# First two feed-forward blocks: eight of the 22 gate and up pairs in each as seven block products

## The chip, the cores and the metric

The kernel runs on one core of a Trainium2 chip. The metric is the device time of one execution in microseconds; smaller is better. TensorE (PE in the profile) multiplies matrices into eight PSUM banks, VectorE (DVE), ScalarE (ACT) and GpSimd (POOL) do the elementwise work, and the queue of SyncE (SP) starts the weight loads.

## The reference, cut to what matters

The program is a chain of transformer-like blocks over 512 tokens of width 1024: a state-space mixer, a feed-forward block, a differential attention, a second feed-forward block, a three-branch mixer, a cross attention, and a third feed-forward block. The change touches the first two feed-forward blocks, which have a short causal convolution over the tokens between the projection and the gate:

```python
def conv_ffn(x, ln_g, up_w, conv_w, conv_b, down_w):
    u = causal_dwconv(rms_norm(x, ln_g) @ up_w, conv_w, conv_b)   # 3 taps
    gate, up = u[..., :FFN_DIM], u[..., FFN_DIM:]                 # FFN_DIM = 2816
    return (jax.nn.silu(gate) * up) @ down_w
```

The third block has the same gate and up projections with no convolution. 2816 columns are 22 tiles of 128, so each block has 22 pairs: one gate tile and one up tile, each a product of a 1024x128 weight with the 1024x512 transposed activations.

## The kernel before, in words

**Order.** A planner (`Plan`) writes out one order of work by hand in ticks. A tick is one piece of TensorE work; every engine's program walks over the same ticks and does what the planner placed there, in order, so each engine is a strict queue whose entries carry an age in ticks. A wait in the middle of a queue holds all that stands behind it.

**Precision.** Each float32 product is made of three float32r products of a rounded high part and a low rest: `wl*xh + wh*xl + wh*xh`. Each unit of weights (128x1024) is loaded by SP into one of three raw buffers, rounded on ACT (`split`, line 1715) and its rest subtracted on DVE (`cut`, line 2230); TensorE waits for the `cut` of the unit (`features`, `quads`).

**An ordinary pair** (`feat` twice) takes 8 ticks: gate in 4 pieces of 6 matmuls of 512 columns, then up likewise, 48 matmuls. Two units are cut. In the first two blocks DVE scales each finished bank into a padded buffer `fu` (`scaled`), ACT makes the first convolution tap of it into `fv`, DVE adds taps 1 and 2 (`SCALAR_TENSOR_TENSOR`, line 2233), ACT makes the silu of the gate, POOL multiplies gate and up (line 2877; DVE for tiles 11 and 21), ACT rounds the result and DVE subtracts the rest (`two_parts`) for the down projection.

**A quad** (`quad`) takes 7 ticks of 12 matmuls of 256 columns, 84 matmuls: a pair regarded as a 2x2 block product (gate and up by the two halves of the 1024 rows; the two halves of the rows by the two halves of the tokens) done by Strassen's seven products p1, p2, p6, p5, p7, p3, p4. Before the change only eleven pairs of the third block are quads. A quad needs four weight units instead of two: the gate weights, two sums of weight blocks (`s1`, `s2`, four additions of 128x512 on DVE at ticks -5 and -3) and half of the up weights. It also needs four combinations of activation blocks ("tees", 4 chunks, made once per block). Its products share three banks: a, b and d. ACT copies the bank b after p1 and after p6, and the bank d after p5, before TensorE may go on in them; DVE reads the bank b after p7 (`q_read`) before p4 may go in.

The waits of TensorE inside a quad are, in `quads`, `cut` of the unit for each product, and

```python
if product == "p6":
    w.wait_ge(*sig["q_copy"].at(f, "p1"))
elif product == "p7":
    w.wait_ge(*sig["q_copy"].at(f, "p6"))
elif product == "p3":
    w.wait_ge(*sig["q_copy"].at(f, "p5"))
elif product == "p4":
    w.wait_ge(*sig["q_read"].at(f))
```

Cut units live in a ring of three buffers. The third unit of a quad, `s2`, is split on ACT in tick 1 of the quad and cut on DVE in tick 2, since its buffer is that of the unit that TensorE left at the end of the tick before the quad; p7 needs it in tick 4.

Of the kernel before, what the change touches and what calls it, by code (L numbers as in the profile page):

```python
# [9 lines left out]
F = mybir.dt.float32  # L10
# [143 lines left out]
QUADS = (4, 5, 7, 8, 10, 12, 13, 15, 16, 18, 19)  # L154
# [7 lines left out]
class Plan:  # L162
# [132 lines left out]
    def quad(self, f, gate, gate_c, up, up_c):  # L295

        key = ("gu", 2, f)
        self.until(lambda: self.past("tees", 3, 6) and self.place(
# [4 lines left out]
        g = Group(key, False, "n2", 0, [], DC, 0, P, H2)  # L303
        sources = (("raw", r, 0, UNIT), ("s1", f, 0, UNIT), ("s2", f, 0, UNIT), ("raw", r + 1, S, S))
# [7 lines left out]
        self.quad_units[f] = (r, *g.units)  # L312
        for u, end in zip(g.units, (("bank", (*key, "a")), ("product", (f, "p5")), ("bank", (*key, "d")),
                                    ("bank", (*key, "b")))):
            self.unit_end[u] = end
        self.start("sum1", f, t - 5)
        self.start("sum2", f, t - 3)
        self.start("quad", f, t)
        src, i = h_of(2, f)
        self.lo[src, i] = t + 11  # L320
# [568 lines left out]
class Buffers:  # L889


    def __init__(self, nc, ctx):
# [41 lines left out]
        self.teeh, self.teel = (t[:, :, :].rearrange("p (i c) (h n) -> p i (c h) n", i=4, h=2) for t in (self.XBh, self.XBl))  # L934
# [126 lines left out]
class Kernel:  # L1061
# [52 lines left out]
    def raw_read(self, r):  # L1114
# [140 lines left out]
def tensor_program(eng, K):  # L1255
# [45 lines left out]
    def quads(p):  # L1301

        g, product = p.group, PRODUCTS[p.k0]
        f = g.key[2]
# [7 lines left out]
        if product == "p6":  # L1312
            w.wait_ge(*sig["q_copy"].at(f, "p1"))
        elif product == "p7":
            w.wait_ge(*sig["q_copy"].at(f, "p6"))
        elif product == "p3":
            w.wait_ge(*sig["q_copy"].at(f, "p5"))
        elif product == "p4":
            w.wait_ge(*sig["q_read"].at(f))
        for k in range(4):  # L1320
            if product == "p1":
                xh, xl = (t[:, 0:H2] for t in buf.operand("n2", k))
                w.wait_ge(*K.ready("n2", k))
            elif product in ("p2", "p3"):
                xh, xl = (t[:, 0:H2] if product == "p2" else t[:, H2:S] for t in buf.operand("n2", 4 + k))
                w.wait_ge(*K.ready("n2", 4 + k))
            else:
                i = ("p5", "p6", "p7", "p4").index(product)
                xh, xl = buf.teeh[:, i, k, :], buf.teel[:, i, k, :]
                w.wait_ge(*sig["tee_lo"].at(k, i))  # L1330
# [3 lines left out]
        t.then_inc(*(fill(key) if QUAD_LAST[name] == product else sig["product"].up(f, product)))  # L1334
# [372 lines left out]

def scalar_program(eng, K):
# [18 lines left out]
    def values(g):  # L1727

        for j in range(g.n):
# [19 lines left out]
            if o == in_bank - 1:  # L1749
                t.then_inc(*leave(key))  # L1750

    ADDED = {"nf": ("out", 3), "nq": ("dn", 0, 1), "nf1": ("ao", 1), "nm": ("dn", 1, 1), "nx": ("mo",), "n2": ("xo", 1),
             "fin": ("dn", 2, 1)}
# [156 lines left out]
    def tees(T):  # L1910
        for k in at("tees", T):
            x_ready("n2", k)
            w.wait_ge(*full(("rs", "n2")))
            w.wait_ge(*sig.par.at())
            if k:
                for i in range(4):
                    w.wait_ge(*sig["tee_lo"].at(k - 1, i))
            copy(K.tee(0), buf.x[:, k, H2:S], pc("ffn2", k)).then_inc(*sig["tee_d"].up(k))
        for k in at("tees", T - 2):
            w.wait_ge(*full(("xo", 1, DC - 1)))  # L1920
            for i, sign in enumerate((1.0, -1.0, 1.0, -1.0)):
                w.wait_ge(*K.tee_ready(k, i))
                copy(buf.teeh[:, i, k, :], K.tee(1 + i), sign).then_inc(*sig["tee_hi"].up(k, i))

    def quads(T):
        for product, age in (("p1", 1), ("p6", 3), ("p5", 4)):
            for f in at("quad", T - age):
                vg, vu = K.quad_rows(f)
                w.wait_ge(*sig["product"].at(f, product))
                if product == "p1":  # L1930
                    w.wait_ge(*K.gated(2, f - 3))
                if product == "p5":
                    w.wait_ge(*sig["lo"].at(*h_of(2, f - 3)))
                out = {"p1": vg[:, 0:H2], "p6": vg[:, H2:S], "p5": vu[:, H2:S]}[product]
                copy(out, K.of(("gu", 2, f, QUAD_BANK[product]))[:, 0:H2]).then_inc(*sig["q_copy"].up(f, product))
        for f in at("quad", T - 7):
            vg, _ = K.quad_rows(f)
            w.wait_ge(*sig["q_row"].at(f))
            func(ACT.Silu, vg[:, :], vg[:, :]).then_inc(*sig["fsilu"].up(2, f))
        for f in at("quad", T - 9):  # L1940
            src, i = h_of(2, f)
            hi, _ = buf.operand(src, i)
            w.wait_ge(*K.gated(2, f))
            if f >= 12:
                w.wait_ge(*full(("dn", 2, 0, DC - 1)))
# [1219 lines left out]
```

## Time and profile before

| | |
|---|---|
| median of 3 runs | 2399.07 us (2397.6 to 2399.99) |
| the profiled execution's own time | 2399.27 us |
| its span, first to last instruction | 2397.5 us |
| PE busy | 2371.2 us, 99% |
| DVE busy | 1484.8 us, 62% |
| ACT busy | 1086.1 us, 45% |
| POOL busy | 357.9 us, 15% |
| TensorE's granted clock, mean | 0.998 of full speed |

An engine is busy while an instruction of its own executes. The span lacks 1.8 us of the execution's time, which lie ahead of the first and behind the last instruction. Shares are means over all stages; what a stage is limited by is read from its own window.

### The profile page before, as it was taken

The page shows a single profiled execution, that of the slowest core. Times are in us where ns is not written, and L with a number is a line of the kernel's source. Part 1 is how long each engine was busy: PE and PEld are TensorE (multiplying, and loading weights), DVE is VectorE, ACT ScalarE, POOL GpSimd, SP SyncE. Part 2 cuts the span into 40 slices and gives each one's busy share as a digit, 9 for nine tenths or more (in the row PEclk, how much of TensorE's full clock was granted, in tenths as well). Part 3 has the DMA queues.
Part 4 walks back from the last instruction along what each step waited for, and adds up shares of the span by engine and source line. Part 5 has one row for each costly group of instructions (what it writes and reads, how often), then busy time and mean ns, then how long its engine had stood idle before and what let it go on. Part 6 is the DMA issues. An engine that isn't in the chain of part 4 may idle for free.

```text
span 2397.5 us, 30764 instructions
## 1 busy us (share of the span) xinstructions
PE 2371.2 (99%) x11952; PEld 1944.2 (81%) x11952; DVE 1484.8 (62%) x2356; ACT 1086.1 (45%) x1878; POOL 357.9 (15%) x286
## 2 busy tenths in 40 slices
PE   8999999999999999999999999999999999999999
PEld 6677878888888877788888877787788878898987
DVE  6778776763666777766456547534655445873763
ACT  6654554442445677644234334324443334442433
POOL 0252252210111000122011100001210001100001
PEclk9999999999999999999999999999999999999999
DMA  4532223223223221232332332231234332233232
GB/s 164 109 93 79 80 70 99 97 86 108 97 83 120 75 76 49 73 108 92 93 106 87 91 131 84 71 102 57 72 123 136 115 106 79 81 105 99 95 97 89
DMA packets 74847, 226.24 MB, mean 94 GB/s; under 512 B 8144, under 2 KB 12368, under 8 KB 74576
## 3 DMA queue, kind: packets, MB, share of 16 engines
q1 hardware_dynamic: 70272, 215.90, 28.1%
q10 hardware_dynamic: 4432, 8.39, 2.0%
q8 instruction: 95, 1.56, 0.3%
q14 instruction: 48, 0.39, 0.1%
HBM read 215.87 MB, written 8.39 MB: 94 GB/s over the span
## 4 chain that ended last, share of the span: by engine, by line
PE 60%; DVE 1%; ACT 0%; issue 0%; DMA 0%; POOL 0%; POOLq 0%; DVEq 0%; ACTq 0%; SPq 0%
PE bank L1272 59%; PE bank L1276 1%; DVE t L2230 1%; DVE t L2233 1%; ACT t L1715 0%; DVE t L2241 0%; DMA t<-in_w 0%; POOL t L2877 0%; ACT t L1718 0%; ACT L1718 0%; DVE t L2237 0%; DVE t L2798 0%; POOLq L3100 0%; DVEq L3100 0%; DVE t L2644 0%
## 5 line engine op out<-in xcount | busy, mean ns | idle before, releaser
L1272 PE MATMUL bank<-t 128*128 128x512 f32 (+5 forms) x11526 | 2346.4, 369 | 19.1 <-DVE t L2233 7.9
L1272 PEld LDWEIGHTS bank<-t 128*128 128x128 f32 (+2 forms) x11526 | 1901.0, 186 | 433.3 <-issue 80.1
L1715 ACT ACTIVATE t<-t 128x1024 fp32r<-128x1024 f32 (+5 forms) x676 | 564.0, 847 | 564.6 <-PE bank L1272 276.6
L2230 DVE TENSOR_TENSOR t<-t 128x1024 fp32r<-128x1024 f32 (+7 forms) x774 | 687.3, 901 | 202.9 <-ACT t L1715 192.4
L1718 ACT ACTIVATE t<-t 128x512 f32<-128x512 f32 (+6 forms) x610 | 367.5, 616 | 455.8 <-DVE t L2230 307.1
L2877 POOL TENSOR_TENSOR t<-t 128x512 f32<-128x512 f32 (+4 forms) x206 | 316.3, 1542 | 1551.9 <-ACT t L1718 559.7
L2230 DVE TENSOR_TENSOR t<-bank,t 128x512 f32<-128x512 f32 (+4 forms) x434 | 279.2, 648 | 425.2 <-PE bank L1272 414.7
L2233 DVE SCALAR_TENSOR_TENSOR t<-t 128x512 f32<-128x512 f32 (+5 forms) x536 | 386.6, 733 | 102.3 <-ACT t L1718 63.8
L1715 ACT ACTIVATE t<-bank 128x512 f32<-128x512 f32 (+4 forms) x184 | 84.7, 477 | 205.4 <-PE bank L1276 146.9
L2880 POOL TENSOR_SCALAR t<-t 128x128 f32<-128x128 f32 (+3 forms) x64 | 40.9, 645 | 478.6 <-ACT t L1715 247.6
L2233 DVE SCALAR_TENSOR_TENSOR t<-bank,t 128x512 f32<-128x512 f32 x56 | 38.5, 688 | 68.8 <-PE bank L1272 68.8
L1276 PE MATMUL bank<-t 128*128 128x128 f32 (+1 forms) x426 | 69.1, 277 | 1.9 <-ACT t L1715 1.2
L1718 ACT ACTIVATE t<-bank,t 128x128 f32<-128x128 f32 (+1 forms) x144 | 42.3, 392 | 44.9 <-DVE t L2798 39.2
L2233 DVE SCALAR_TENSOR_TENSOR t<-t,bank 128x512 f32<-128x512 f32 x40 | 28.4, 710 | 54.2 <-PE bank L1272 51.7
L2241 DVE CUSTOM_DVE_ANT_0 t<-bank,t 128x256 f32<-128x256 f32 (+3 forms) x128 | 55.7, 462 | 9.8 <-PE bank L1272 7.5
L1276 PEld LDWEIGHTS bank<-t 128*128 128x128 f32 (+1 forms) x426 | 50.0, 141 | 14.4 <-issue 4.2
L1718 ACT ACTIVATE t<-bank 128x512 f32<-128x512 f32 (+3 forms) x73 | 38.5, 539 | 13.4 <-PE bank L1272 8.5
L2237 DVE TENSOR_SCALAR t<-t 128x256 f32<-128x256 f32 (+6 forms) x88 | 33.6, 383 | 2.9
L1715 ACT ACTIVATE t<-bank,t 128x256 f32<-128x256 f32 (+1 forms) x32 | 15.3, 524 | 21.9 <-PE bank L1272 18.7
L1718 ACT ACTIVATION_READ_ACCUMULATOR t<-t 128x1 f32 x128 | 24.4, 191 | 0.0
L1718 ACT ACT_TABLE_LOAD x11 | 14.1, 1283 | 0.2
L2238 DVE TENSOR_SCALAR t<-bank 128x4 f32<-128x4 f32 (+1 forms) x14 | 2.2, 159 | 16.8 <-PE bank L1272 16.8
(30 smaller groups left out, 53.0 us busy)
## 6 DMA issues: line engine op xcount, KB each, us to landing
t<-in_w SPq DMA_DIRECT2D x304, 512.0 KB, 3.4
t<-in_w SPq DMA_DIRECT2D x48, 384.0 KB, 3.0
t<-in_w SPq DMA_DIRECT2D x56, 320.0 KB, 3.0
t<-in_w SPq DMA_DIRECT2D x28, 256.0 KB, 2.8
tab<-t ACTq DMA_DIRECT2D x1, 2560.0 KB
t<-in_x SPq DMA_DIRECT2D x8, 256.0 KB, 5.0
t<-tab SPq DMA_DIRECT2D x8, 256.0 KB, 3.7
spill<-t ACTq DMA_DIRECT2D x1, 2048.0 KB, 8.3
```

The lines of the kernel that those rows point to most:

```text
L1272: return eng.matmul(out, lhs, rhs, start=start, stop=stop, skip_group_check=loose)
L1276: return eng.transpose(out, in_, ident[0:n, 0:n])
L1715: return eng.activation(out, in_, ACT.Copy, scale=scale)
L1718: return eng.activation(out, in_, f, bias=bias, scale=scale, accum_out=accum)
L2230: return eng.tensor_tensor(out, a, b, o)
L2233: return eng.scalar_tensor_tensor(out=out, in0=a, scalar=s, in1=b, op0=o0, op1=o1)
L2237: return eng.tensor_scalar(out, a, s0, None, o0)
L2238: return eng.tensor_scalar(out, a, s0, s1, o0, o1)
L2241: return eng.tensor_tensor_reduce(out, a, b, 1.0, FMAX, ADD, MIN, m)
L2877: return eng.tensor_tensor(out, a, b, o)
L2880: return eng.tensor_scalar(out, a, s, s1, o, o1)
```

## The change

Pairs 5, 7, 9, 12, 14, 16, 18 and 20 of blocks 0 and 1 become quads; the third block keeps its eleven. So between two new quads stands one ordinary pair (two before the down projections of tiles 0 to 11, pairs 10 and 11). The combinations of activations are made for the first two blocks too, in the 4 MB (XAh, XAl) that are free there, with 6 ticks from chunk to chunk (4 in the third block). The convolution stays in a quad: DVE scales the assembled rows into `fu` (the up half with a factor -1), then ACT and DVE make the taps for gate and up, DVE makes the product of gate and up that POOL makes for an ordinary pair.

```diff
-QUADS = (4, 5, 7, 8, 10, 12, 13, 15, 16, 18, 19)
+QUADS = {0: (5, 7, 9, 12, 14, 16, 18, 20), 1: (5, 7, 9, 12, 14, 16, 18, 20), 2: (4, 5, 7, 8, 10, 12, 13, 15, 16, 18, 19)}
...
-        self.lo[src, i] = t + 11
+        self.lo[src, i] = t + (11 if s == 2 else 14)
...
-        if s == 2:
-            for k in range(4):
-                self.once("tees", k, lambda k=k: self.past("rms", "n2", 3) and (k == 0 or self.past("tees", k - 1, 4)))
+        apart = 4 if s == 2 else 6
+        for k in range(4):
+            self.once("tees", (s, k), lambda k=k: self.past("rms", src, 3) and (
+                k == 0 or self.past("tees", (s, k - 1), apart)))
...
-                if s == 2 and f in QUADS:
-                    self.quad(f, gate, gate_c, up, up_c)
+                if f in QUADS[s]:
+                    self.quad(s, f, gate, gate_c, up, up_c)
                     continue
...
-        self.teeh, self.teel = (t[:, :, :].rearrange("p (i c) (h n) -> p i (c h) n", i=4, h=2) for t in (self.XBh, self.XBl))
+        self.tees = [tuple(t[:, :, :].rearrange("p (i c) (h n) -> p i (c h) n", i=4, h=2) for t in pair)
+                     for pair in ((self.XAh, self.XAl), (self.XAh, self.XAl), (self.XBh, self.XBl))]
```

On ACT, in `quads`:

```diff
+        for kind, age in (("ga", 7), ("up", 8)):
+            for s, f in at("quad", T - age):
+                if s == 2:
+                    continue
...
+                w.wait_ge(*(sig["q_row"] if kind == "ga" else sig["q_up"]).at(s, f))
...
+                func(ACT.Identity, buf.fv[n % 6][:, :], buf.fu[n % 3][:, 2:S + 2], pc(f"fcb{s}", ft),
+                     pc(f"fcw{s}", 3 * ft)).then_inc(*sig["tap0"].up((kind, s, f)))
+        for age in (10, 7):
+            for s, f in at("quad", T - age):
+                if age == (10 if s < 2 else 7):
...
+                    func(ACT.Silu, vg[:, :], vg[:, :]).then_inc(*sig["fsilu"].up(s, f))
+        for age in (12, 9):
...
+                    copy(hi, K.quad_rows(f)[1][:, :], 1.0 if s < 2 else -1.0).then_inc(*sig["hi"].up(src, i))
```

On DVE, in `quads`:

```diff
+            if s < 2:
+                fu_free(2 * f, s)
+                tt(buf.fu[2 * f % 3][:, 4:S + 4], vg[:, :], row[:, :], MUL).then_inc(*sig["q_row"].up(s, f))
...
+            if s < 2:
+                out = buf.fu[(2 * f + 1) % 3][:, 4:S + 4]
+                fu_free(2 * f + 1, s)
+                stt(out[:, H2:S], vu[:, H2:S], -1.0, row[:, H2:S], MUL, MUL).then_inc(*sig["q_up"].up(s, f))
+                w.wait_ge(*full(("gu", s, f, "b")))
+                stt(out[:, 0:H2], b, -1.0, row[:, 0:H2], MUL, MUL).then_inc(*leave(("gu", s, f, "b")))
...
+        for kind, age in (("ga", 8), ("up", 9)):
+            for s, f in at("quad", T - age):
+                if s < 2:
+                    taps((kind, s, f))
+        for age in (11, 8):
+            for s, f in at("quad", T - age):
+                if age == (11 if s < 2 else 8):
...
+                    tt(vu[:, :], vu[:, :], vg[:, :], MUL).then_inc(*sig["fmul_last"].up(s, f))
+        for age in (13, 10):
...
+                    if s < 2:
+                        tt(lo, K.quad_rows(f)[1][:, :], hi.bitcast(F), SUB).then_inc(*sig["lo"].up(src, i))
...
+    def taps(key):
...
+        for k in (1, 2):
+            w.wait_ge(*(sig["tap0"].at(key) if k == 1 else sig["tap"].at(key, 1)))
+            stt(v[:, :], ub[:, 2 + k:S + 2 + k], pc(f"fcw{s}", 3 * ft + k), v[:, :], MUL, ADD).then_inc(
+                *sig["tap"].up(key, k))
```

## Rows read from the trace of the kernel before

**Rows 1.** The page: span, engines, granted clock, chain that ended last

```profile
span 2397.5 us, 30764 instructions
...
PE 2371.2 (99%) x11952; PEld 1944.2 (81%) x11952; DVE 1484.8 (62%) x2356; ACT 1086.1 (45%) x1878; POOL 357.9 (15%) x286
...
PEclk9999999999999999999999999999999999999999
...
PE 60%; DVE 1%; ACT 0%; issue 0%; DMA 0%; POOL 0%; POOLq 0%; DVEq 0%; ACTq 0%; SPq 0%
```

**Rows 2.** Critical chain in time order, first-block stretch: start us, us, what

```profile
1033.38 360.24 PE bank L1272 x1592
```

**Rows 3.** Windows: us, PE, PEld, DVE, ACT, POOL busy, PEclk, DMA share, GB/s

```profile
1060.00:1125.30 65.30, 65.30 (x290) 54.07 (x289) 44.00 (x55) 28.84 (x38) 13.23 (x6) 1.00 0.31 98
2228.00:2240.00 12.00, 12.00 (x101) 11.90 (x100) 9.70 (x16) 6.80 (x11) 0.00 (x0) 1.00 0.29 89
2257.40:2288.60 31.20, 31.20 (x217) 29.20 (x216) 26.18 (x37) 14.48 (x22) 1.68 (x1) 1.00 0.33 102
```

**Rows 4.** DVE groups by form, 440 to 505.28 us (first block, ordinary pairs)

```profile
L2233 DVE SCALAR_TENSOR_TENSOR t<-t 128x512 f32<-128x512 f32 x25 | 18.8, 752 | 7.8 <-ACT t L1718 7.3
L2230 DVE TENSOR_TENSOR t<-t 128x1024 fp32r<-128x1024 f32 x12 | 14.6, 1219 | 0.0
```

**Rows 5.** DVE groups by form, 2226.2 to 2288.6 us (third block, two periods)

```profile
L2230 DVE TENSOR_TENSOR t<-t 128x512 f32<-128x512 f32 x24 | 17.2, 730 | 1.1
L2230 DVE TENSOR_TENSOR t<-bank,t 128x256 f32<-128x256 f32 x16 | 6.7, 420 | 4.5 <-PE bank L1272 4.5
L2230 DVE TENSOR_TENSOR t<-bank,t 128x512 f32<-128x512 f32 x4 | 2.8, 688 | 3.5 <-PE bank L1272 3.5
```

**Rows 6.** DVE in time, first block: start us, us, what, xcount, idle before

```profile
477.87 1.54 DVE L2233 SCALAR_TENSOR_TENSOR t<-t 128x512 f32<-128x512 f32 x2 [0.22 <-ACT t L1718]
479.32 1.22 DVE L2230 TENSOR_TENSOR t<-t 128x1024 fp32r<-128x1024 f32 x1
```

**Rows 7.** DVE, then POOL, in time, third block

```profile
2258.27 2.39 DVE L2230 TENSOR_TENSOR t<-t 128x512 f32<-128x512 f32 x2
...
2270.88 1.22 DVE L2230 TENSOR_TENSOR t<-t 128x1024 fp32r<-128x1024 f32 x1
2272.01 0.68 DVE L2233 SCALAR_TENSOR_TENSOR t<-t 128x512 fp32r<-128x512 f32 x1
...
2258.44 1.68 POOL L2877 TENSOR_TENSOR t<-t 128x512 f32<-128x512 f32 x1 [116.19 <-DVE t L2230]
```

**Rows 8.** ACT groups by form, 2226.2 to 2288.6 us

```profile
L1715 ACT ACTIVATE t<-t 128x1024 fp32r<-128x1024 f32 x16 | 16.6, 1047 | 0.0
L1715 ACT ACTIVATE t<-bank 128x256 f32<-128x256 f32 x12 | 4.6, 383 | 15.1 <-PE bank L1272 15.1
```

**Rows 9.** ACT groups by form, 440 to 505.28 us

```profile
L1718 ACT ACTIVATE t<-t 128x512 f32<-128x512 f32 x18 | 13.6, 754 | 18.7 <-DVE t L2230 14.3 <-DVE t L2233 3.9
```

**Rows 10.** All engines in time, entry into the third block's first quad

```profile
2083.06 7.25 PEld L1272 LDWEIGHTS bank<-t 128*128 128x128 f32 x60 [1.87 <-DVE t L2230]
```

**Rows 11.** DVE in time, one chunk of tees' low parts, third block

```profile
2066.60 1.42 DVE L2233 SCALAR_TENSOR_TENSOR t<-t 128x256 fp32r<-128x256 f32 x4
```

**Rows 12.** DVE in time, ordinary pair of the first block

```profile
476.95 0.69 DVE L2230 TENSOR_TENSOR t<-t 128x512 fp32r<-128x512 f32 x1
```

**Rows 13.** DMA issues by line: size of one, median us to landing

```profile
t<-in_w SPq DMA_DIRECT2D x304, 512.0 KB, 3.4
```

More of the change, by code:

```diff
@@ L293, in feat_steps, with quad @@
         self.pending.append(g)
-    def quad(self, f, gate, gate_c, up, up_c):
-        key = ("gu", 2, f)
-        self.until(lambda: self.past("tees", 3, 6) and self.place(
+    def quad(self, s, f, gate, gate_c, up, up_c):
+        key = ("gu", s, f)
+        self.until(lambda: self.past("tees", (s, 3), 6) and self.place(
             [((*key, "b"), 0, 10), ((*key, "a"), 1, 4), ((*key, "d"), 3, 6)]), key)
@@ L311, in quad @@
             self.put(Piece(g, i // 2, i, i + 1, i == 0))
-        self.quad_units[f] = (r, *g.units)
-        for u, end in zip(g.units, (("bank", (*key, "a")), ("product", (f, "p5")), ("bank", (*key, "d")),
+        self.quad_units[s, f] = (r, *g.units)
+        for u, end in zip(g.units, (("bank", (*key, "a")), ("product", (s, f, "p5")), ("bank", (*key, "d")),
                                     ("bank", (*key, "b")))):
             self.unit_end[u] = end
[L316 to L319, printed above, removed]
-        self.lo[src, i] = t + 11
+        self.start("sum1", (s, f), t - 5)
+        self.start("sum2", (s, f), t - 3)
+        self.start("quad", (s, f), t)
+        src, i = h_of(s, f)
+        self.lo[src, i] = t + (11 if s == 2 else 14)
     def halves(self, key, name, c, src, nk, row0, per, after):
@@ L1910, in tees @@
     def tees(T):
-        for k in at("tees", T):
-            x_ready("n2", k)
-            w.wait_ge(*full(("rs", "n2")))
+        for sk in at("tees", T):
+            s, k = sk
+            src = FFN_IN[s]
+            x_ready(src, k)
+            w.wait_ge(*full(("rs", src)))
             w.wait_ge(*sig.par.at())
@@ L1916, in tees @@
                 for i in range(4):
[L1917 to L1920, printed above, removed]
+                    w.wait_ge(*sig["tee_lo"].at((s, k - 1), i))
+            copy(K.tee(0), buf.x[:, k, H2:S], pc(GAINS[src], k)).then_inc(*sig["tee_d"].up(sk))
+        for sk in at("tees", T - 2):
+            s, k = sk
+            teeh, _ = buf.tees[s]
+            w.wait_ge(*full((*ADDED[FFN_IN[s]], DC - 1)))
@@ L1936, in quads @@
[L1936 to L1945, printed above, removed]
-            copy(hi, K.quad_rows(f)[1][:, :], -1.0).then_inc(*sig["hi"].up(src, i))
+                copy(out, K.of(("gu", s, f, QUAD_BANK[product]))[:, 0:H2]).then_inc(*sig["q_copy"].up(s, f, product))
@@ L2505, in quads @@
             w.wait_ge(*K.loaded(r + 1))
[L2506 to L2512 removed]
+            if before:
+                w.wait_ge(*sig["cut"].at(before[2]))
@@ L2513, in quads @@
+            tt(buf.s1[:, S:UNIT], b[:, 0:S], b[:, S:UNIT], ADD).then_inc(*sig["sum1"].up(sf))
+            w.wait_ge(*sig["sum1"].at(sf))
+            tt(buf.s1[:, 0:S], a[:, 0:S], buf.s1[:, S:UNIT], ADD).then_inc(*sig["sum"].up(*sf, "s1"))
+        for sf in at("sum2", T):
+            r, before = plan.quad_units[sf][0], K.sums_before(sf)
             a, b = buf.raws[r % N_W], buf.raws[(r + 1) % N_W]
-            if f != QUADS[0]:
-                w.wait_ge(*sig["cut"].at(plan.quad_units[QUADS[QUADS.index(f) - 1]][3]))
+            if before:
+                w.wait_ge(*sig["cut"].at(before[3]))
@@ L2524, in quads @@
-        for f in at("quad", T - 5):
+            w.wait_ge(*full(("gu", s, f, "a")))
+            w.wait_ge(*sig["q_copy"].at(s, f, "p1"))
+            tt(vg[:, 0:H2], K.of(("gu", s, f, "a"))[:, 0:H2], vg[:, 0:H2], ADD).then_inc(*leave(("gu", s, f, "a")))
+        for s, f in at("quad", T - 5):
             _, vu = K.quad_rows(f)
-            w.wait_ge(*sig["product"].at(f, "p7"))
-            w.wait_ge(*sig["q_copy"].at(f, "p5"))
-            tt(vu[:, H2:S], K.of(("gu", 2, f, "b"))[:, 0:H2], vu[:, H2:S], ADD).then_inc(*sig["q_read"].up(f))
@@ L2529, in quads @@
[L2529 removed]
+            w.wait_ge(*sig["product"].at(s, f, "p7"))
+            w.wait_ge(*sig["q_copy"].at(s, f, "p5"))
+            tt(vu[:, H2:S], K.of(("gu", s, f, "b"))[:, 0:H2], vu[:, H2:S], ADD).then_inc(*sig["q_read"].up(s, f))
+        for s, f in at("quad", T - 6):
             vg, _ = K.quad_rows(f)
[L2531 to L2537 removed]
@@ L2551, in quads @@
-        for f in at("quad", T - 10):
-            src, i = h_of(2, f)
-            hi, lo = buf.operand(src, i)
-            w.wait_ge(*sig["hi"].at(src, i))
-            stt(lo, K.quad_rows(f)[1][:, :], -1.0, hi.bitcast(F), MUL, SUB).then_inc(*sig["lo"].up(src, i))
+            row = K.rms_row(FFN_IN[s])
+            w.wait_ge(*full(("gu", s, f, "d")))
+            tt(vg[:, H2:S], K.of(("gu", s, f, "d"))[:, 0:H2], vg[:, H2:S], ADD).then_inc(*leave(("gu", s, f, "d")))
+            w.wait_ge(*empty(("rb", FFN_IN[s])))
```

194 lines of the change are left out of this document (106 added, 88 removed).

## The prediction

> **What bounds the kernel now.** I read the page first: PE is busy 99% of the span at full clock, and the chain that ended last runs over PE's matmuls; DVE has 62%, ACT 45%, POOL 15% [rows 1]. The chain in order of time then shows that the feed-forward stretch is one unbroken run of matmuls [rows 2]. So time falls only if TensorE gets less to do, and rises as soon as TensorE waits. The windows give its prices. In the first block's ordinary pairs 65.30 us hold 290 matmuls of 512 columns, one or two of them only overlapping the edges: 0.2267 us each. In a quad of the third block 12.00 us hold 101 of 256 columns: 0.120 us each [rows 3]. The same rows show the other side: DVE is busy 44.00 of 65.30 us in ordinary pairs (67%), and 26.18 of 31.20 us (84%) where two quads and a pair alternate [rows 3].
>
> **What TensorE saves.** A pair costs 48 x 0.2267 = 10.88 us, a quad 84 x 0.120 = 10.08 us, so 0.80 us are saved each, 12.8 us over 16. A matmul of half the columns costs 53%, not 50%, and there are 7/8 of the columns.
>
> The Trainium skill (TensorE: Matmul & The Clock Gate, section "Wait — 56ns, not 53.3ns?") puts a warm matmul at its columns by 2.4 GHz plus some 2.5 ns. By that a pair would be 10.36 us and a quad 9.17 us, and the saving 19 us, an estimate from that page; the rows disagree (226.7 and 120 ns against 215.8 and 109.2), and since both forms are measured here, in this kernel's own loops, the rows decide.
>
> **What DVE gets to do.** I take a period of one new quad and one ordinary pair, 15 ticks: TensorE needs 10.08 + 10.88 = 20.96 us. DVE's part:
> - Ordinary pair: 44.00 / 6 = 7.33 us [rows 3]. It holds two cuts of 1.22 us, four taps of 0.75 [rows 4], two evictions of 0.69 [rows 5] and the rest of 0.69 [rows 12]; neighbours overlap by 0.08. The two taps of a bank take 1.45 us from start to next start, 1.42 of it busy [rows 6]; without taps the pair is 7.33 - 2.84 = 4.49.
> - POOL's product of gate and up, once a period: while it ran in the third block, two DVE instructions of 512 took 2.39 us together [rows 7], where 2 x 0.69 less the overlap is 1.3. So it costs a loaded DVE 1.05 us; the mean of 24 such, 730 against 688 ns [rows 5], says the same.
> - Quad of the third block: (26.18 - 4.49 - 1.05) / 2 = 10.32 us. Three and a half cuts, four additions for the sums, three additions of 256 columns, scaling, product and rest are in it.
> - The new quads add the taps of gate and up, 2.84 us: 13.16. Their product of gate and up is on DVE in the third block as well. The form with a factor of -1 takes the place of a plain one; no row here has it with a bank of 256 columns, and between a plain one of 0.42 [rows 5] and a tap of 0.75 for twice the columns [rows 4] the difference is under 0.1 us each; I take 0, and 0.2 a period for the high end.
>
> Sum: 13.16 + 7.33 + 1.05 = 21.54 us of busy DVE, 103% of TensorE's 20.96. DVE becomes the bound of the alternating stretches. Two forced idles come on top. After the eviction of the up bank DVE has one addition (0.33) to do before it needs ACT's first tap (0.75 [rows 9]): 0.35 with the semaphores. After the gate row it has two of 256 (0.7) against ACT's 0.75: 0.1. So a period is 22.0 us, and a saturated one stalls TensorE for 22.0 - 20.96 = 1.05 us. Before, two pairs took 21.76.
>
> **Where TensorE waits.** The tight entry is the cut of `s2`: its buffer comes free only as the quad begins, and p7 needs it in tick 4, 4 x 12 x 0.120 = 5.76 us later. In the first new quad DVE is on time. From its tick 8 (11.3 us, when the gate row and the first tap are there) to tick 13 the queue holds, from start to next start, two times taps and cut (2.58 each), sums (1.3 and 1.27), eviction and product (1.27), rest, taps and cut (3.2): 12.2 us. It ends at 23.5, 2.55 into the next quad. Then eviction 0.61, ACT's tap 0.75, taps 1.45, cut 1.13 and some 0.05: 6.55 against 5.76. Quad 7 stalls 0.8, quad 9 1.05. The first quad behind the down projections, 12, has no pair ahead whose taps it must carry, so 14 stalls 0.35 and 16, 18, 20 stall 1.05 each. That is 1.85 + 3.5 = 5.35 per block, 10.7 for both. After 9 and after 20 a lag remains of under 3 us; pairs 10 and 11, where DVE is at 67%, and the missing sums behind quad 20 take it in: 0.
>
> **The other edits.** The four chunks of tees are eight DVE operations of 256 each: four rests take 1.42 us [rows 11], four combinations as much, so 2.9 a chunk, 11.4 a block, ahead of quad 5. TensorE's pairs leave DVE 3.55 us each, 17.7 in five, so they fit, but with the first evictions, that come in one lump, up to 1 us of lag reaches quad 5. In the third block the first quad's start waited 1.87 us for DVE [rows 10], with 4 ticks between chunks and two quads in a row; here I take 0.5 per block, 1.0 in all (0 to 3.8). ACT gets 1.5 splits of 1.05 us and three copies of 0.38 more per quad [rows 8]; with 44% of its time used in ordinary pairs [rows 3] it reaches some 55%, hidden by itself, but it stands in the same chain: its copy of p1 is queued behind the silu that waits for DVE's taps, and by the ledger above ends 0.1 to 0.3 us before p6 needs it. If that cover goes, the price is the same lag, not a second one. Weight loads stay the same bytes; a load of 3.4 us [rows 13] is started when DVE has cut or summed a buffer, some 7 us ahead of its next use, since no two new quads are neighbours. The down projection gets its operand three ticks later in the plan, with a pair behind every quad. All 0.
>
> **Sum.** -12.8 + 10.7 + 1.0 = -1.1 us against the profiled execution's 2399.27 (span 2397.5 [rows 1]); that time is 0.2 above the median of the runs shown, so 2398.0 on its scale: no change that can be told, since about 0.2%, 4.8 us, is what a measurement of this kernel can tell from none.
>
> **Rivals.**
> - *DVE keeps up (faster).* Without POOL's 1.05 the busy time is 20.5, below 20.96, and the idles fall in the 0.5 left. For it: TensorE lost only 31.20 - 168 x 0.120 - 48 x 0.2267 = 0.16 us in a period of two quads at 84% [rows 3], and POOL may fall where DVE waits anyway. Against: in the saturated queue the cut of half a unit and its like follow POOL's start at once. Stalls would be 16 x 0.08 and 1.0 at the entries, 2.3: 12.8 - 2.3 = 10.5 us faster, 2388.6. It decides below 20.96 of DVE per period. Chance 0.30. The Trainium skill (SBUF — State Buffer, "Who interferes with whom") says that GpSimd and a DVE instruction with two SBUF inputs lock each other out for the whole instruction, and that one with a single SBUF input is free; the 2.39 us agree. By that rule POOL costs nothing if additions out of banks follow it, which is this rival.
> - *ACT and DVE wait for each other (slower).* The mechanism is the chain in two strict queues: POOL's late product holds ACT's rounding, behind which stands the split of the next unit, which DVE's cut waits for (0.2 to 0.4 us), besides dependent neighbours (0.04 each, five of them) and the longer form with -1 (0.2). The period is then 22.8: saturated stalls 1.84, the first ones 0.8 longer: 3.4 + 6.7 per block, 20.2 for both, and 1.0: 8.4 us slower, 2407.5. It decides from some 1.5 us per saturated stall. For it: with 84% DVE still idled for ACT and TensorE in turn. Chance 0.22.
> - *The entries cost what the third block's does.* 3.8 instead of 1.0: 2400.8. Chance 0.04, on top of the forecast's 0.44.
>
> **How the numbers follow.** The forecast's own range is a period of 21.7 to 22.3 us, 12 x 0.3 = 3.6 us either way, 2394.5 to 2402. The 8-in-10 range takes in both rivals' numbers, 2388.5 to 2408. Faster by over 0.2% is the first rival and the low edge of the forecast: 0.32; within 0.45; slower 0.23.
>
> **What the profile after would show.** PE: 1344 more matmuls of 256 columns and 768 fewer of 512. In pairs 14 to 20 of the first two blocks DVE busy above 95%, with waits of TensorE for DVE (the cut, before p7) of about 1 us per quad, none of that size in quads 5 and 12. Four to six waits of ACT in a row would speak for the second rival; DVE under 92% and stalls of 0.1 for the first. I am wrong if TensorE's waits come from ACT's copies, from the loads, or from the entry.

## The result and the profile after

The changed kernel takes 2413.19 us in the median (4 runs, 2412.21 to 2414.16), the kernel before 2399.53 beside it (4 runs, 2397.6 to 2400.66): a ratio of 1.006, 95% interval 1.0045 to 1.0075. It is slower by 13.7 us, outside the predicted range of 2388.5 to 2408.

The page of the changed kernel, the same parts as [rows 1]:

```profile
span 2411.7 us, 32441 instructions
...
PE 2366.2 (98%) x12528; PEld 1965.2 (81%) x12528; DVE 1616.3 (67%) x2596; ACT 1133.2 (47%) x1998; POOL 325.0 (13%) x270
...
PE 53%; DVE 7%; ACT 1%; issue 1%; DMA 0%; POOL 0%; DVEq 0%; POOLq 0%; ACTq 0%; SPq 0%
```

PE has 576 matmuls more, as was worked out, and 5 us less of busy time where 12.8 were: part of TensorE's waiting is counted as busy, as the sums below show. DVE now holds 7% of the chain that ended last, where it held 1%. DVE is busy 131 us longer.

Who TensorE waited for, in the whole span (engine and line, total us, times, longest):

```profile
PE bank L1281 <- DVE t L2262: 22.6, 19, 2.9
```

L2262 is the line of the cut and of DVE's other operations on two inputs (L2230 before); 17 of the 19 waits, 19.8 us, are in blocks 0 and 1. A block's length can be read from the starts of its matmuls, since their number is known. Blocks 0 and 1 took 359.8 and 359.9 us before and 366.9 and 367.2 after; the attention in between 255.9 and 255.8. So the two blocks hold the loss, 14.4 us; the other stages vary by up to 1.5 us between kernels in which they are the same.

Windows of the changed kernel, as [rows 3]: the stretch from pair 0 to the entry of quad 7, then single periods of a new quad and a pair:

```profile
417.50:482.60 65.10, 60.26 (x304) 51.02 (x303) 60.90 (x91) 36.31 (x59) 11.15 (x5) 1.00 0.26 81
672.50:694.90 22.40, 21.38 (x134) 19.23 (x134) 21.26 (x30) 11.68 (x18) 2.20 (x1) 1.00 0.29 94
1295.30:1317.70 22.40, 21.38 (x135) 19.22 (x134) 21.26 (x31) 11.68 (x18) 2.20 (x1) 1.00 0.30 95
```

A period is 22.4 us with 21.26 us of busy DVE, against 22.0 and 21.54 predicted. The first window is the surprise: DVE is busy 60.90 of 65.10 us before the alternation has begun. The kernel before in the same stretch:

```profile
417.30:482.60 65.30, 65.30 (x292) 54.12 (x290) 47.20 (x58) 30.96 (x40) 12.63 (x6) 1.00 0.29 93
```

So DVE's first pairs were fuller than the 44.00 us of [rows 3] already. Ahead of quad 5 alone, 43.4 us from 417.5, DVE was idle for 11.0 us before and is for 3.1 after. TensorE's waits in that stretch stand in the order of time (start us, us, what, idle before):

```profile
439.73 14.67 PE L1281 MATMUL bank<-t 128*128 128x512 f32 x64
455.29 8.56 PE L1281 MATMUL bank<-t 128*128 128x512 f32 x48 [0.89 <-DVE t L2262]
466.76 3.13 PE L1281 MATMUL bank<-t 128*128 128x256 f32 x24 [2.92 <-DVE t L2262]
470.93 4.34 PE L1281 MATMUL bank<-t 128*128 128x256 f32 x34 [1.04 <-DVE t L2262]
```

From the starts of the matmuls these waits are worth 1.1, 3.1 (ahead of p6) and 1.4 us with the slower matmuls right behind each: 5.6 per block. Quads 7, 9, 16, 18 and 20 wait 1.39 us each, all but 0.1 of it ahead of p7, quad 14 0.73, quad 12 nothing: 7.7 per block. So 26.6 us of waits in two blocks stand against 12.8 us saved. (The trace counts 19.8 of the 26.6 as idle, the rest as busy.)

### The profile page after: what moved, and what is told of

Read it like the earlier page. It is cut to its first block, busy times and chain, and to the rows that moved or that the text cites. A ratio compares the mean times of both kernels' runs of the same rounds, so it can differ in the third digit from the quotient of the medians.

```text
span 2411.7 us, 32441 instructions
## 1 busy us (share of the span) xinstructions
PE 2366.2 (98%) x12528; PEld 1965.2 (81%) x12528; DVE 1616.3 (67%) x2596; ACT 1133.2 (47%) x1998; POOL 325.0 (13%) x270
## 4 chain that ended last, share of the span: by engine, by line
PE 53%; DVE 7%; ACT 1%; issue 1%; DMA 0%; POOL 0%; DVEq 0%; POOLq 0%; ACTq 0%; SPq 0%
PE bank L1281 52%; DVE t L2262 4%; DVE t L2265 3%; PE bank L1285 1%; ACT t L1733 1%; ACT t L1730 0%; DVE t L2273 0%; DMA t<-in_w 0%; POOL t L2945 0%; ACT L1733 0%; DVE t L2269 0%; DVE t L2866 0%; POOLq L3168 0%; DVEq L3168 0%; DVE t L2712 0%
## 5 line engine op out<-in xcount | busy, mean ns | idle before, releaser
L1281 PE MATMUL bank<-t 128*128 128x512 f32 (+3 forms) x12102 | 2341.7, 359 | 38.4 <-DVE t L2262 22.6
L1281 PEld LDWEIGHTS bank<-t 128*128 128x128 f32 (+1 forms) x12102 | 1922.4, 187 | 426.7 <-issue 82.6
L2262 DVE TENSOR_TENSOR t<-t 128x1024 fp32r<-128x1024 f32 (+8 forms) x902 | 792.3, 897 | 197.1 <-ACT t L1730 184.5
L1730 ACT ACTIVATE t<-t 128x1024 fp32r<-128x1024 f32 (+8 forms) x748 | 603.5, 824 | 565.2 <-PE bank L1281 269.2
L2262 DVE TENSOR_TENSOR t<-bank,t 128x512 f32<-128x512 f32 (+3 forms) x450 | 276.0, 620 | 339.2 <-PE bank L1281 327.3
L2945 POOL TENSOR_TENSOR t<-t 128x512 f32<-128x512 f32 (+3 forms) x190 | 283.5, 1500 | 1600.5 <-ACT t L1733 578.0
L2265 DVE SCALAR_TENSOR_TENSOR t<-t 128x512 f32<-128x512 f32 (+3 forms) x616 | 423.1, 703 | 76.7 <-ACT t L1733 37.3
L1730 ACT ACTIVATE t<-bank 128x256 f32<-128x256 f32 (+4 forms) x232 | 102.6, 455 | 219.3 <-PE bank L1285 145.2
L2265 DVE SCALAR_TENSOR_TENSOR t<-bank,t 128x512 f32<-128x512 f32 (+1 forms) x72 | 45.2, 628 | 67.2 <-PE bank L1281 67.2
L1285 PEld LDWEIGHTS bank<-t 128*128 128x128 f32 (+1 forms) x426 | 49.7, 140 | 14.2 <-issue 3.9
L1733 ACT ACTIVATE t<-bank 128x512 f32<-128x512 f32 (+3 forms) x73 | 38.5, 539 | 13.7 <-PE bank L1281 8.5
```

What stands on the lines that cost most here:

```text
L1281: return eng.matmul(out, lhs, rhs, start=start, stop=stop, skip_group_check=loose)
L1285: return eng.transpose(out, in_, ident[0:n, 0:n])
L1730: return eng.activation(out, in_, ACT.Copy, scale=scale)
L1733: return eng.activation(out, in_, f, bias=bias, scale=scale, accum_out=accum)
L2262: return eng.tensor_tensor(out, a, b, o)
L2265: return eng.scalar_tensor_tensor(out=out, in0=a, scalar=s, in1=b, op0=o0, op1=o1)
```

## The experiments

Waits below are sums over a quad of what the matmuls' starts lie further apart than 0.120 or 0.2267 us. (Some expectations have 0.57 or 0.58 us for a wait that this count gives as 0.48.) Block lengths are those of blocks 0 and 1. Where a run has one time only, the block lengths carry the verdict.

### Is it the combinations, the entry, or the alternation?

```diff
# tees_only
+QUADS = {0: (), 1: (), 2: (4, 5, 7, ...)}
# entry_alone
+QUADS = {0: (5,), 1: (12,), 2: (4, 5, 7, ...)}
# from7
+QUADS = {0: (7, 9, 12, 14, 16, 18, 20), 1: (7, 9, 12, 14, 16, 18, 20), 2: ...}
```

> No new quads; the four chunks of activation combinations are still made in blocks 0 and 1 and used by nobody. Theory A (DVE's queue is full while they are made, 3.9 us a chunk with POOL's locks): TensorE loses about 1 us per block, near tile 3, as it does before the first quad in the changed kernel: 2 us over the kernel before, 2401 to 2402. Rival (the combinations cost nothing, the stall at the entry is all the first quad's own): equal to before within 0.5 us.

Measured: 2403.28 beside 2398.66; blocks 360.9 and 361.0 us, one wait of 1.1 in each. Theory A. Of the rest, 1.5 us lie in the third block, whose code is unchanged.

> Block 0 has one new quad, pair 5; block 1 has one, pair 12. Theory A: pair 5 meets the lag that the combinations left on DVE, so block 0 loses 5.5 us in waits and gains 0.8; block 1 loses 1.05 ahead and gains 0.8 with a quad that waits for nothing. Together 5 us over before, about 2404.5. Rival (waits come from alternation alone, quads that follow each other): a quad by itself waits for nothing, block 0 looks like block 1, and the time is within 1 us of before.

Measured: block 0 364.9 us, with waits of 1.1 and 4.7; block 1 360.3, with 1.1 and none at quad 12. Theory A, to 0.4 us. The whole took 2414.37, 10 us more than forecast, and 9 of them lay in the attention, which is unchanged: 264.9 us instead of 255.9.

> Quads 7, 9, 12, 14, 16, 18, 20: pair 5 stays an ordinary pair in blocks 0 and 1, the rest is the changed kernel. Theory A (lag of DVE behind the combinations, worked off at 3.5 us per ordinary pair): the 4.5 us wait of the first quad goes and quad 7 waits 0.6 instead of 1.4; 9 us less than the changed kernel, about 2404. Rival (the first quad of a block always waits, as in the third block, for its own sums and weight loads): the wait moves to quad 7 and the time stays at 2412 to 2414.

Measured: blocks 363.4 us, 3.6 less than in the changed kernel: the long wait ahead of quad 5 is gone, but quad 7 waits 1.45, not 0.6, so theory A has the place of the lag right and the rate at which it is worked off wrong. The whole took 2412.60, since the attention had 263.7 us.

The common feature of these two is an odd number of new quads in block 0, so the attention begins at another parity of the plan's ticks, and in the planner its heads may start on even ticks only:

```diff
# one_tick: the kernel before, with
 def diff(self):
+    self.put()
     self.start("diff", 0)
```

> The kernel before, with one empty tick in the plan ahead of the attention stage and nothing else. The two runs with an odd number of new quads in block 0 had attention stages of 264 and 265 us where all with an even number had 256. If the cause is that the planner starts heads on even ticks, so that its whole order there depends on the parity of the tick it begins at, this kernel takes 8 us more, 2406. If it was the quads or TensorE's clock, it takes what before takes.

Measured: 2404.21 beside 2397.92. The attention stage in windows, before and then with the tick:

```profile
771.30:1027.20 255.90, 252.32 (x1398) 200.75 (x1396) 187.87 (x410) 174.27 (x370) 30.58 (x43) 1.00 0.24 75
```

```profile
771.20:1035.60 264.40, 254.38 (x1399) 201.24 (x1398) 188.15 (x410) 175.49 (x372) 28.73 (x43) 0.99 0.23 73
```

The second window begins some 0.8 us of work earlier, since the last six matmuls of block 0 now come behind the norm. From the first matmul of block 0 to that of block 1 it is 615.6 and 623.4 us: the tick costs 7.7. Parity is shown as the cause. Behind block 1 two stages gave 3.5 us back: the mixer 1.5, a difference that it also has between other kernels, and the cross attention, whose heads start on even ticks too, 1.9 (159.3 us instead of 161.3). The comparisons below keep the parity of the attention; that of the cross attention is kept in all but the last.

### Is the entry DVE's content?

```diff
# entry_short_taps, in taps()
+m = 64 if f < 5 else S
+stt(v[:, 0:m], ub[:, 2 + k:m + 2 + k], ..., v[:, 0:m], MUL, ADD)
```

> The changed kernel with both taps of tiles 0 to 4 of blocks 0 and 1 done for 64 of 512 tokens (the rest lacks them): 1.87 us less of DVE per ordinary pair ahead of quad 5, 9 us in all, nothing else. If the entry's wait is DVE's content (lag behind the combinations), the 1.05 and the 3.1 us ahead of quad 5 go, and only its 1.2 ahead of p7 stays: blocks of 362 to 363 us for 367, about 2404. If the first quad waits for its own sums or loads, the 3.1 us stay, 2411.

Measured: 2402.66 beside 2397.95, blocks 361.2 and 361.4 us. All waits up to and at quad 5 are gone, its 1.2 ahead of p7 as well, which the forecast had left standing: the short taps of pair 4 are queued ahead of the cut that p7 needs. The same window as above holds 65.10 us of busy PE:

```profile
417.50:482.60 65.10, 65.10 (x336) 55.84 (x335) 57.28 (x99) 38.30 (x63) 7.36 (x5) 1.00 0.26 84
```

So the entry is content. DVE of the changed kernel shows what the prediction missed there:

```profile
446.05 1.22 DVE L2262 TENSOR_TENSOR t<-t 128x1024 fp32r<-128x1024 f32 x1
447.18 2.83 DVE L2265 SCALAR_TENSOR_TENSOR t<-t 128x256 f32<-128x256 f32 x4
449.93 0.68 DVE L2262 TENSOR_TENSOR t<-bank,t 128x512 f32<-128x512 f32 x1
450.53 1.42 DVE L2265 SCALAR_TENSOR_TENSOR t<-t 128x256 fp32r<-128x256 f32 x4
...
456.63 1.54 DVE L2265 SCALAR_TENSOR_TENSOR t<-t 128x512 f32<-128x512 f32 x2 [0.89 <-ACT t L1733]
```

The kernel before has four combinations while POOL rests (third block):

```profile
2063.75 1.80 DVE L2233 SCALAR_TENSOR_TENSOR t<-t 128x256 f32<-128x256 f32 x4
```

So of the 2.83 us here 1.80 are the combinations' own, not the 1.42 of four rests of the same width that the prediction took, and 1.03 came from POOL's product (446.21 to 448.41), which had its lock in them. Behind two of the banks DVE stood 0.89 us for ACT's first tap. A lag that is made there is not worked off at the rate at which DVE was idle before, since part of that idleness is such waits.

### Throughput or the order of the queues?

```diff
# short_tap_quad
+m = 64 if k == 2 and f in QUADS[s] else S
# short_tap_pair
+m = 64 if kind == 'up' and (f + 1 in QUADS[s] or f == 10) else S
```

> In the new quads the last convolution tap is done for 64 of the 512 tokens only (the rest lacks it), for gate and for up: 0.93 us less of DVE per period, at ticks 8 and 9 of the quad, nothing else. Theory A (throughput: the period is the content of DVE's queue, 22.4 us): the wait per quad falls from 1.39 to about 0.5, in quads 16, 18, 20 too. Theory B (latency: the wait is the chain eviction, ACT's tap, taps, cut of s2 that begins with the quad; the 0.93 are not in it): it stays at 1.4.

Measured: 2404.57 beside 2398.66; 0.48 us in every quad from 7 on but quad 12, which waits for nothing; blocks 363.3 and 362.3. Most of the 1.39 is throughput. That the rest is the same everywhere, in quad 14 as in quad 20, was the first sign of a floor.

> The counterpart of the run with short last taps in the new quads: there the wait per quad fell from 1.39 to 0.57 us. Now both taps of the up half of the ordinary pair ahead of each new quad are done for 64 of 512 tokens (the rest lacks them): the same 0.93 us less of DVE per period, but at tick 2 of the quad, inside the chain eviction, ACT's tap, taps, cut of s2. Theory A (throughput): the same 0.5 to 0.6 us per quad, blocks 0 and 1 at 363 us each. Theory B (latency of that chain): it would have to do better than the quad's short taps, down to 0.4 or less, since B held them for nothing.

Measured: 2418.68 and blocks 369.1 us. Less work, and the wait grew to 1.7 us per quad. Neither theory said so. DVE of that run around a quad's tick 4, and POOL:

```profile
700.14 0.61 DVE L2265 SCALAR_TENSOR_TENSOR t<-t 128x64 f32<-128x64 f32 x2 [0.56 <-ACT t L1733]
701.09 2.71 DVE L2262 TENSOR_TENSOR t<-t 128x1024 fp32r<-128x1024 f32 x2 [0.34 <-ACT t L1730]
704.99 0.42 DVE L2262 TENSOR_TENSOR t<-bank,t 128x256 f32<-128x256 f32 x1 [1.19 <-PE bank L1281]
...
700.83 1.29 POOL L2946 TENSOR_TENSOR t<-t 128x512 f32<-128x512 f32 x1 [21.39 <-DVE t L2265]
```

The changed kernel at the same place, 5.8 us into a quad:

```profile
677.98 2.91 DVE L2262 TENSOR_TENSOR t<-t 128x1024 fp32r<-128x1024 f32 x2
678.14 2.20 POOL L2945 TENSOR_TENSOR t<-t 128x512 f32<-128x512 f32 x1 [20.17 <-DVE t L2265]
```

Both groups of two are the cut of s2 and a rest of 512 columns, which take 1.22 and 0.68 us in product_dve. The short taps let POOL begin at 700.83, ahead of the cut at 701.09, so the cut waits for POOL and takes 2.11. In the changed kernel the cut was first and took 1.22, POOL waited, and the rest behind the cut, which TensorE doesn't need, took 1.78. DVE pays about 1 us in either order; the lock's place decides what that costs TensorE. The Trainium skill (SBUF — State Buffer, "Who interferes with whom") says that the order of issue, not the form of the instructions, decides which of the two blocks, and the trace agrees (2.11 and 1.22 us for the same cut).

```diff
# product_dve: in blocks 0 and 1 DVE does the ordinary pairs' gate * up
-if g.key[0] == "up" and ... and g.key[2] in LAST_UP:
+if g.key[0] == "up" and ... and (g.key[1] < 2 or g.key[2] in LAST_UP):
# cut_first: s2 ahead of the pair's first tap on ACT, ahead of its taps on DVE
 quads(T)
+for u in plan.split_at.get(T - 1, ()):      # DVE: plan.cut_at.get(T, ())
+    if early(u):                            # s2 of a quad of blocks 0, 1
+        split(u)                            # DVE: cut(u)
 ffn(T)
```

> In blocks 0 and 1 DVE multiplies gate and up of the ordinary pairs too (0.61 us) and POOL does nothing there; same results. If POOL's lock costs a full DVE 1.05 us per product, a saturated quad waits 0.44 less, 0.95 us instead of 1.39, and the entry 1 to 2 us less per block: blocks of 363.5 us for 367.0, about 2406. If POOL's instruction costs DVE nothing, DVE gets 0.61 more per period: waits of 2.0 us and about 2422.

Measured: 2411.30, blocks 365.2 and 365.4. The entry lost 1.2 us of wait, but a saturated quad still waits 1.3, which neither forecast said. The period has 20.66 us of busy DVE and is 22.3 us long. DVE behind the cut of s2:

```profile
677.29 2.42 DVE L2262 TENSOR_TENSOR t<-t 128x1024 fp32r<-128x1024 f32 x3
680.30 0.42 DVE L2262 TENSOR_TENSOR t<-bank,t 128x256 f32<-128x256 f32 x1 [0.59 <-PE bank L1281]
```

It ends its work earlier and then waits 0.59 us for p7, which TensorE could begin only when s2 was cut. POOL's lock had lain beside p7, at no cost to the loop.

> Same work in another order: in the first ticks of a new quad ACT splits s2 ahead of the pair's first tap, and DVE cuts s2 ahead of the pair's taps. Theory A (throughput): only the 0.56 us that DVE stands idle for ACT's tap is filled, the wait falls from 1.39 to 0.8 to 1.1 us, where it turns up may change. Theory B (the late entry is the cut of s2 behind the taps): it is 1.45 us earlier, the wait goes to 0 to 0.2 us, about 2399.

Measured: 2411.74, blocks 367.0. The wait ahead of p7 is gone, but 0.34 us stand ahead of p6 and 1.0 ahead of the next pair's gate; the period is 22.35. So at eight quads neither edit alone takes the wait of a saturated quad away.

### Fewer quads

```diff
# sparse: and apart = 8 in place of 6
+QUADS = {0: (7, 10, 12, 15, 18, 20), 1: (7, 10, 12, 15, 18, 20), 2: ...}
# four_cut_first: apart = 8, cut_first, and
+QUADS = {0: (8, 12, 15, 18), 1: (8, 12, 15, 18), 2: ...}
# sparse_cut_first: sparse with cut_first
# cut_first_short: cut_first with short_tap_quad
```

> New quads 7, 10, 12, 15, 18, 20 in blocks 0 and 1 (an even number, so that the ticks of the attention keep their parity), two ordinary pairs between most of them, the chunks of combinations 8 ticks apart. DVE then has 28 of 32 us per quad and two pairs. Theory A: the waits are under 0.2 us per quad, except for quad 20 with one pair ahead, and each of the 12 quads keeps most of its 0.80 us: blocks of 355.5 to 356.5 us against 359.8 before, 7 to 8.5 us faster than before, 2391. If quads lose time for another reason (their form), the blocks stay at 360 or above.

Measured: 2399.46 beside 2397.45, ratio 1.0007 (0.9997 to 1.0017); blocks 360.2 and 360.3, not 355.5 to 356.5. Quad 7 waits 2.2 us, 20, with one pair ahead, 1.4, 12, behind the down projections, nothing; quads 10, 15 and 18 wait 0.48 us each though DVE has slack. DVE, then PE, at quad 15:

```profile
636.75 0.68 DVE L2262 TENSOR_TENSOR t<-bank,t 128x512 f32<-128x512 f32 x1
638.68 0.42 DVE L2262 TENSOR_TENSOR t<-bank,t 128x256 f32<-128x256 f32 x1 [1.25 <-PE bank L1281]
639.03 1.53 DVE L2265 SCALAR_TENSOR_TENSOR t<-t 128x512 f32<-128x512 f32 x2
640.47 2.92 DVE L2262 TENSOR_TENSOR t<-t 128x1024 fp32r<-128x1024 f32 x2
...
635.72 5.80 PE L1281 MATMUL bank<-t 128*128 128x256 f32 x47
641.74 1.46 PE L1281 MATMUL bank<-t 128*128 128x256 f32 x10 [0.22 <-DVE t L2262]
```

DVE stands 1.25 us at the addition that needs p2; the pair's taps and the cut of s2 are queued behind it, and the cut ends 6.1 us after the quad's start, not before 5.76.

> Four new quads per block, 8, 12, 15, 18, never fewer than two ordinary pairs apart, the first one 24 ticks behind the last combination's start, chunks 8 ticks apart, and s2 split and cut ahead of the pair's taps. If both waits found so far are all there is (0.6 us per quad because the cut of s2 stands behind an addition that needs p2 and behind the taps; 0.8 more where DVE has no slack), every quad keeps its 0.80 us: blocks of 356.6 to 357 us against 359.8, 5.5 to 6.5 us faster than before. If the 0.6 us have another cause, the blocks are at 359 and the time is that of before.

Measured: 2397.74 beside 2397.92, ratio 0.9998 (0.9989 to 1.0007); blocks 359.2. A wait of 0.86 us stands behind each quad but 12. POOL, then ACT, then DVE, at quad 15:

```profile
638.33 1.68 POOL L2957 TENSOR_TENSOR t<-t 128x512 f32<-128x512 f32 x1 [11.20 <-DVE t L2274]
...
640.04 1.58 ACT L1733 ACTIVATE t<-t 128x512 fp32r<-128x512 f32 x2 [1.53 <-POOL t L2957]
...
641.66 1.23 DVE L2271 TENSOR_TENSOR t<-t 128x1024 fp32r<-128x1024 f32 x1 [0.26 <-ACT t L1733]
```

ACT waits for POOL's product, and the split of the next gate unit is queued behind: the chain of the prediction's slower rival.

> The run with quads 7, 10, 12, 15, 18, 20 with s2 split and cut ahead of the pair's taps, nothing else. There quads 10, 12, 15 and 18 waited 0.58 us ahead of p7 although DVE had slack, and 7 and 20 waited 2.0 and 1.4. Floor theory (the cut of s2 stands behind the addition that needs p2, and behind the taps): the 0.58 go to nothing, 20 keeps a wait of 0.8 to 1, wherever it turns up; blocks of 357.3 us for 360.2. Pure throughput theory: nothing changes, 360.

Measured: 2401.05, blocks 361.3, 1.1 more than without, where the floor theory had 357.3. The 0.48 went, 0.86 came.

> All eight new quads, s2 split and cut ahead of the pair's taps, and the last tap of the new quads done for 64 of 512 tokens. With the short taps alone the wait was 0.57 us, which is the floor if it comes from the order, or what is left of throughput if it does not. Floor theory: 0 to 0.3 us per quad from 7 on, 16 quads, blocks of 359.5 us. Pure throughput: 0.5 to 0.6 us as before, blocks of 362 to 363.

Measured: 2408.21, blocks 364.0 and 364.4: every quad from 7 on but 12 waits 0.86. The floor is not DVE's content, and moving one link of the chain alone doesn't remove it.

### Both links at once

```diff
# all_cf_dve: cut_first and product_dve
# four_cf_dve: the same with apart = 8 and
+QUADS = {0: (8, 12, 15, 18), 1: (8, 12, 15, 18), 2: ...}
# six_cf_dve, and six_timed, which is the same kernel: apart = 8 and
+QUADS = {0: (7, 10, 12, 15, 18, 20), 1: (7, 10, 12, 15, 18, 20), 2: ...}
```

> Quads 8, 12, 15, 18 with s2 split and cut first, chunks 8 ticks apart, and the ordinary pairs' product of gate and up on DVE instead of POOL in blocks 0 and 1. With s2 first the wait had moved to the gate unit of the next pair, 0.86 us each, behind this chain: POOL's product (1.7 us with its lock), ACT's rounding, the split that is queued behind it, the cut. If that chain is the cause, the product on DVE (0.6) ends the wait: each quad keeps its 0.80 us, blocks of 356.6 to 357 us against 359.8 before and 359.2 with POOL, 5 to 6.5 us faster than before. If the wait is DVE's content, 0.6 us more of it per pair leave it at 0.86 or longer and the time at 2397 to 2400.

Measured: 2391.66 (9 runs) beside 2397.05, ratio 0.9975 (0.9965 to 0.9985); blocks 356.6 and 356.7, no wait at all at the quads. The chain that begins with POOL's product was the cause.

> Quads 7, 10, 12, 15, 18, 20 with the same two edits. Chain theory: 10, 15, 18 wait for nothing, 12 neither, 7 keeps its 0.9 us ahead of p6 from the lag behind the combinations, 20 with one pair ahead at most 0.5: blocks of 356.5 us (360.2 and 361.3 with POOL). If POOL's chain is not it: 360 or more.

Measured: blocks 355.6 and 355.7, 2390.0. The chain theory, and 0.9 us per block better than its forecast: quad 7 waits for nothing either. In sparse_cut_first, which differs by POOL's product alone, it waited 0.95 ahead of p6, so POOL's product was part of the lag behind the combinations.

> All eight new quads with the two edits. Neither order nor POOL can delay TensorE now, what is left is DVE's content: 21.26 busy in the changed kernel, less 1.05 for the lock, plus 0.61 for the product, plus the short idles: a period of 21.1 to 21.5 us, a wait of 0.2 to 0.5 per quad instead of 1.39. The entry of quad 5 keeps most of its 4 us, since it is content too. Blocks of 361 us, 2400 to 2401. If each period has a floor of its own that these edits don't touch, the waits stay at 1.2 to 1.4 and the blocks at 365.

Measured: 2395.54, blocks 358.4 and 358.5, better than forecast: the entry's waits are 0.4 and 2.7 us. The two edits that took off 1.7 us per block and nothing when made alone take off 8.6 together. A period in the windows:

```profile
664.20:685.50 21.30, 21.22 (x133) 19.14 (x132) 20.66 (x31) 11.65 (x18) 0.00 (x0) 1.00 0.30 99
```

21.3 us with 20.66 of busy DVE: at most 0.33 us of wait per quad instead of 1.39. product_dve has the same 20.66 and a period of 22.3: the order alone is worth 1.0.

> Quads 7, 10, 12, 15, 18, 20, s2 first, product on DVE, as before, now timed: blocks of 355.6 us against 359.8, so 8.5 us less in the two blocks, less up to 1.5 us in which the third block's entry and TensorE's clock vary: 6 to 8 us faster than before, a ratio of 0.997.

Measured: 2392.06 (8 runs) beside 2397.95, ratio 0.9973 (0.9963 to 0.9984): 5.9 us faster, just under the forecast.

```diff
# seven_cf_dve: cut_first, product_dve, apart = 8, and
+QUADS = {0: (7, 9, 12, 14, 16, 18, 20), 1: (7, 9, 12, 14, 16, 18, 20), 2: ...}
 if h == 1:
+    if s == 0:
+        self.put()
```

> Quads 7, 9, 12, 14, 16, 18, 20 with the two edits and chunks 8 ticks apart; one empty tick ahead of the down projections of block 0 keeps the parity of the attention's ticks. Seven times 0.80 less some 0.33 for 9, 16, 18 and 20: blocks of 355.2 to 355.6 us, the same as with six quads within 0.5 us, 7 to 8 us faster than before. If the alternation still had a cost of its own, it would be slower than six by over 2 us.

Measured: 2387.57 (5 runs) beside 2397.95, ratio 0.9955 (0.9943 to 0.9968): 10.4 us faster than the kernel before and 25.6 less than the change as made. Blocks 355.2 and 355.7:

```profile
410.80:766.00 355.20, 355.06 (x1842) 305.49 (x1842) 273.67 (x398) 169.49 (x248) 11.35 (x8) 1.00 0.30 97
```

The window holds hardly a break, but the starts show waits of 0.15 to 0.32 us at quads 9, 16, 18 and 20. Against six quads 4.5 us less was measured where the blocks say 0.4. Of the rest, by the two profiled executions, 1.9 lie in the cross attention, 159.3 us instead of 161.3, as with one_tick: seven quads in block 1 shift its first tick by an odd number, so this part of the gain is parity and not the quads'. Another 1.5 lie in the third block and come and go with TensorE's clock (see below).

## Why the prediction was wrong

**TensorE's saving** was right: an undisturbed quad is 83 steps of 119.9 ns, and four_cf_dve keeps all but 0.1 of it, 3.2 us in a block with four quads.

**The entry** is the step that failed most: "so they fit ... here I take 0.5 per block". It was 5.6 us per block, 10 us too little in the sum. Three prices were left out of a queue that had become full. POOL's lock was counted once per period in the alternation and not at all ahead of it. The combinations were taken at 1.42 us a chunk, where a row of the kernel before has 1.80: 1.5 us per block. And the slack was too large: 3.55 us a pair make 14.2 for the four pairs ahead of quad 5, where DVE had 11.0 idle before, 2.3 of them waits for ACT's first tap, with which no lag can be worked off ([rows 4] has 7.3 of these in six pairs). entry_short_taps shows that the entry is content, and product_dve that the lock is 1.2 us of it; how the rest divides was not measured. The prediction named waits from the entry as a sign that it is wrong, and 11.2 of the 26.6 us are that.

**The period** was right in kind and in DVE's busy time, 21.26 against 21.54, but the forced idles were 1.1 us, not 0.45, so a saturated quad waits 1.39 instead of 1.05. But the period isn't simply content and idles: in product_dve the content fell by 0.6 and the period by 0.1. The step "In the first new quad DVE is on time" failed: I let the cut of s2 stand behind the pair's taps but these behind nothing, while an addition that needs p2 is ahead of them. Every quad with a pair ahead whose taps it must carry has this floor of 0.48 us, and quad 7 waits as long as quad 9. Together 15.4 us of waits where 10.7 were forecast. Entry and period account for the miss: -12.8 + 15.4 + 11.2 = 13.8 us.

**POOL's lock of 1.05 us** was measured rightly, but adding it to the period was wrong in this order of work: it lay beside p7 and cost nothing there (product_dve), and moved ahead of the cut it held the cut up by 0.9 (short_tap_pair). That the period came out near, 22.0 for 22.4, is in part luck: a cost was added that wasn't there, and idle was left out that was.

**The rivals.** The slower one named a chain that is there, POOL's product, ACT's rounding, the split behind it, but in the changed kernel it wasn't what TensorE waited for: its 0.86 us came up only when the cut of s2 was moved ahead. Its period of 22.8 was 0.4 too long, and it took the entry at 1.0 too, so that 2407.5 lies nearer by too large a price for the one and too small a price for the other. "DVE keeps up" fell: the changed kernel's DVE is full wherever quads alternate. Its condition, under 20.96 us of DVE per period, was wrong as well: product_dve had 20.66, and TensorE waited 1.3 per quad. The entry rival, at 3.8 us, had the right place and a third of the size. What the prediction said of loads, of the down projections' operand and of ACT's copies held: no wait of TensorE in the two blocks of the changed kernel is put down to them. (The ordinary pairs that the prediction calls the first block's, [rows 2] and the first window of [rows 3], lie in block 1; the two blocks differ by 0.1 us.)

**Of TensorE's clock:** after the wait of 1.9 us at the third block's entry the changed kernel ran 3.4 us at 1.2 GHz (2096.9 to 2100.3, granted 0.55 in the window's mean), which the profiled run of before did not; matmuls of 256 columns were 213 ns apart. It costs some 1.4 us: from its first pair to the end the third block takes 353.8 us without such a stretch and 355.2 with it. It comes in some executions and not in others: six_timed and six_cf_dve are one kernel with the same wait, and only the first has it (granted 0.58 from 2075.5 to 2078.9). It doesn't explain the loss.

## What to carry to other kernels

When the engine with slack takes over work from the bound one, add up its queue for the worst stretch, with the stretch ahead of it, not for the mean: a lag is worked off only with idleness that isn't itself a wait. Then find, for each thing that the bound engine needs early, what stands ahead of it in every strict queue; one deadline inside a loop costs the same however little work the loop holds (0.48 us with one pair between quads and short taps, and with two pairs), and moving one link moves the wait to the next. If an order is planned in ticks, check that a stage further down doesn't depend on their parity.

## What the runs showed of the hardware

- A GpSimd product of 128x512, 1.29 us long when DVE leaves it alone (before), cost DVE about 1 us in either order. Where it began 0.26 us ahead of a cut of 128x1024, the cut took 2.11 us (short_tap_pair); where the cut began 0.16 us ahead, the cut took 1.22, GpSimd's product 2.20 and DVE's next instruction 1.78 instead of 0.68 (the changed kernel).
- Four fp32 combinations of 128x256 took 1.80 us with GpSimd idle, four rests of the same width 1.42 (before).
- Less work made the kernel slower: 0.93 us less of DVE per period, 0.3 us more of wait per quad (short_tap_pair).
- One empty tick in a plan, in which no engine does anything, cost 7.7 us in the attention stage (one_tick). This is the plan's doing, not the chip's.
